# Decoder layer with a 32-expert MoE: biases kept resident and picked by a one-hot product, expert weights read in pairs of 4 MB

## What is computed

```python
logits = h.astype(jnp.float32) @ lw['w_router'].astype(jnp.float32) + lw['b_router'].astype(jnp.float32)
top_v, top_e = lax.top_k(logits, TOP_K)
gate = jax.nn.softmax(top_v, axis=-1).astype(h.dtype)
...
def run_block(args):
    xb, e = args
    gu = xb @ lw['w_gu'][e] + lw['b_gu'][e]
    gt = jnp.minimum(gu[:, :D_EXPERT], SWIGLU_LIMIT)
    up = jnp.clip(gu[:, D_EXPERT:], -SWIGLU_LIMIT, SWIGLU_LIMIT)
    act = (up + 1.0) * gt * jax.nn.sigmoid(SWIGLU_ALPHA * gt)
    return act @ lw['w_dn'][e] + lw['b_dn'][e]
```

## Time and profile before

| | us |
|---|---|
| median of 3 executions | 1600.88 (1596.57 to 1605.15) |
| the profiled execution, its own time | 1600.38 |
| its span in the trace | 1598.6 |
| TensorE busy in it | 1516.3 |
| VectorE, ScalarE busy | 482.5, 333.9 |
| items of the mixture of experts | from 640 to 1581 |

### The profile page before, as it was taken

The page is one execution under the profiler, slowest core; times in us unless marked ns, Lnnn a source line. Parts: engine busy times, 40 slices in busy tenths (PEclk is TensorE's granted clock), DMA queues, the critical chain, the costliest instruction groups (busy, mean ns, idle before and its releaser), DMA issues.

```text
span 1598.6 us, 24684 instructions
## 1 busy us (share of the span) xinstructions
PE 1516.3 (95%) x9777; PEld 797.6 (50%) x9777; DVE 482.5 (30%) x1079; ACT 333.9 (21%) x795; POOL 6.8 (0%) x13
## 2 busy tenths in 40 slices
PE   6999889999999999999999999999999999999996
PEld 4888885776677687333333333333333333333332
DVE  1566556323301024321222222222212212212224
ACT  2333551223311102111111111121111111111113
POOL 0000000000000000000000000000000000000000
PEclk8999999999999998999999999999999999999999
DMA  9748443534589964799999999999999999999991
GB/s 396 327 158 333 208 160 123 232 129 124 178 315 375 355 257 156 289 396 428 428 428 429 428 428 429 428 428 429 428 429 427 429 428 427 427 420 425 428 417 66
DMA packets 60258, 541.31 MB, mean 339 GB/s; under 512 B 7298, under 2 KB 11906, under 8 KB 29346
## 3 DMA queue, kind: packets, MB, share of 16 engines
q1 hardware_dynamic: 59474, 534.65, 81.3%
q0 software_dynamic: 720, 5.76, 0.9%
HBM read 533.54 MB, written 6.84 MB: 338 GB/s over the span
## 4 chain that ended last, share of the span: by engine, by line
PE 67%; DMA 21%; DVE 6%; issue 3%; SPq 2%; ACT 1%; ACTq 0%; DVEq 0%
DMA regC<-biases 20%; PE banks L605 14%; PE banks L558 10%; PE banks L1321 9%; PE banks L872 5%; PE banks L576 2%; PE banks L1154 2%; PE banks L508 2%; PE banks L1086 2%; PE banks L970 2%; DVE regA L693 2%; PE banks L533 2%; DMA ring<-wpre 1%; PE banks L805 1%; PE banks L1179 1%
## 5 line engine op out<-in xcount | busy, mean ns | idle before, releaser
L558 PE MATMUL banks<-ring,regA 128*64 128x512 f32 x2024 | 446.9, 594 | 0.7 <-ACT regA L630 0.7
L558 PEld LDWEIGHTS banks<-ring,regA 128*64 128x64 f32 x2024 | 142.5, 137 | 281.7 <-issue 280.7
L605 PE MATMUL banks<-ring,regC 128*64 128x512 f32 x1024 | 226.8, 595 | 1.4
L667 DVE TENSOR_TENSOR regB<-regB,banks 128x528 f32<-128x528 f32 x128 | 81.5, 699 | 334.1 <-PE banks L533 334.1
L605 PEld LDWEIGHTS banks<-ring,regC 128*64 128x64 f32 x1024 | 71.6, 137 | 136.0 <-issue 127.7
L633 ACT ACTIVATE regA<-regA 128x512 f32<-128x512 f32 x32 | 20.2, 631 | 538.0 <-DVE regA L688 538.0
L688 DVE TENSOR_SCALAR regA<-banks 128x512 f32<-128x512 f32 x32 | 22.1, 692 | 357.4 <-PE banks L576 357.4
L508 PE MATMUL banks<-regC,regA 128*64 128x512 f32 (+1 forms) x396 | 109.9, 677 | 0.0
L872 PE MATMUL banks<-hT,ring 128*128 128x264 f32 x384 | 86.5, 387 | 0.0
L872 PEld LDWEIGHTS banks<-hT,ring 128*128 128x128 f32 x384 | 72.6, 190 | 12.8 <-issue 0.4
L533 PE MATMUL banks<-regA,regC 64*128 64x264 f32 x512 | 71.6, 409 | 0.0
(11 more groups left out here) (476 smaller groups left out, 1538.0 us busy)
## 6 DMA issues: line engine op xcount, KB each, us to landing
ring<-w_gu SPq DMA_DIRECT2D x126, 2048.0 KB, 17.7
ring<-w_dn SPq DMA_DIRECT2D x64, 2048.0 KB, 15.0
ring<-wpre SPq DMA_DIRECT2D x41, 2048.0 KB, 13.3
ring<-kvT SPq DMA_DIRECT2D x64, 256.0 KB, 4.8
ring<-kv SPq DMA_DIRECT2D x64, 256.0 KB, 6.0
ring<-ssm SPq DMA_DIRECT2D x2, 2048.0 KB, 15.2
o_ssms<-ring POOLq DMA_DIRECT2D x2, 2048.0 KB, 8.2
regC<-w_gu SPq DMA_DIRECT2D x1, 2048.0 KB, 10.8
```

The lines of the kernel that those rows point to most:

```text
L558: mm = pe_mm(bank[x // 2][SLOT * (x % 2):SLOT * (x % 2 + 1), :], lhsT=hg[:, k % 4, SLOT * (k // 4):SLOT * (k // 4 + 1)], rhs=weights_k[:, ...
L605: mm = pe_mm(bank[5][SLOT * y:SLOT * (y + 1), :], lhsT=actT[:, m % 4, SLOT * (m // 4):SLOT * (m // 4 + 1)], rhs=ring[c][:, D * (m % 4) + H ...
L667: V.tensor_tensor(pair, pair, banks[:, b:b + 2, 0:T], ALU.add).then_inc(acc_added, 1)
```

## The change

- The six buffers become one tensor `ring_all`, so that two neighbours can be written as one pair of 4 MB: `pair[0]` is c0 and c1, `pair[1]` c2 and c3, `pair[2]` c4 and c5. From item 3 on, and for c2 to c5 of item 2, one DMA fills a pair, with rows of 32 KB. A pair is refilled when TensorE has read both its halves. Item 2 is written out too, so the loops of SP and TensorE start at 3.
- `w_dn` is read as rows 8p to 8p+7 in partition p, 32 KB in one piece. The intermediate columns follow: half y is now columns 8n + 4y + q, so the moving operand of the gate and up products (`own_columns`) takes 4 numbers, skips 4, takes 4.
- `brow` holds the gate and up biases of all 32 experts (two DMAs at the start, 2 x 128 KB); `load_bias` is gone. A stationary operand `pick` (64 partitions x 64), ones in expert e's row of each half, is made by one VectorE instruction an item, and the bias product is `pick` times `brow` over 32 partitions instead of one.
- `owner` says which expert an item has: two small copies of the identity at the start, one more copy and one small product for further items.

```diff
-        ring = [sb(f"ring{i}", [P, CH]) for i in range(RING)]
+        ring_all = sb("ring_all", [P, RING * CH])
+        ring = [ring_all[:, CH * i:CH * (i + 1)] for i in range(RING)]
+        pair = [ring_all[:, 2 * CH * i:2 * CH * (i + 1)] for i in range(RING // 2)]
...
-        wdn = t["w_dn"].rearrange("e (c p r) n -> e c p (r n)", c=2, p=P)
+        wdn = t["w_dn"].rearrange("e (p r) n -> e p (r n)", p=P)
+        def own_columns(v, y):
+
+            return v.rearrange("p (n y q) -> p n y q", y=2, q=4)[:, :, y, :]
+
...
-            def load_bias(e):
-                for u in range(2):
-                    sp.dma_start(brow[32 * u:32 * u + 1, :].rearrange("a (h n) -> a h n", h=2),
-                                 t["biases"][bass.ds(e, 1), :, HALF * u:HALF * (u + 1)]).then_inc(brow_in, 16)
+            def load_pair(i, e):
+                src = wgu[bass.ds(e, 1), :, 2 * CH * i:2 * CH * (i + 1)] if i < 2 else wdn[bass.ds(e, 1), :, :]
+                sp.dma_start(pair[i], src.rearrange("a p n -> p (a n)")).then_inc(slot_in[2 * i], 16)
...
-            load_bias(0)
-            def later_chunks(j, e):
-                for c in range(1, RING):
-                    sp.wait_ge(moe_read, j * 6 + (c - 5))
-                    load(c, e)
-                load_bias(e)
-
-            def first_chunk(j, e):
-                sp.wait_ge(moe_read, j * 6 - 5)
-                load(0, e)
+            for u in range(2):
+                sp.dma_start(brow[NE * u:NE * (u + 1), :].rearrange("e (h n) -> e h n", h=2),
+                             t["biases"][:, :, HALF * u:HALF * (u + 1)]).then_inc(stage("rest_in"), 16)
+
+            def later_pairs(j, e):
+                for i in range(1, 3):
+                    sp.wait_ge(moe_read, j * 6 + (2 * i - 4))
+                    load_pair(i, e)
+
+            def first_pair(j, e):
+                sp.wait_ge(moe_read, j * 6 - 4)
+                load_pair(0, e)
...
-            load_bias(1)
-
-            with sp.Fori(2, NE - 1) as j:
-                later_chunks(j, j)
-                first_chunk(j + 1, j + 1)
-            later_chunks(NE - 1, NE - 1)
+
+            sp.wait_ge(moe_read, 8)
+            load(1, 2)
+            later_pairs(2, 2)
+            first_pair(3, 3)
+            with sp.Fori(3, NE - 1) as j:
+                later_pairs(j, j)
+                first_pair(j + 1, j + 1)
+            later_pairs(NE - 1, NE - 1)
...
-                                       rhs=weights_k[:, HALF * x:HALF * (x + 1)],
+                                       rhs=own_columns(weights_k[:, D * (x // 2):D * (x // 2 + 1)], x % 2),
...
-                pe.wait_ge(brow_in, j * 32 + 32)
                 pe.wait_ge(acc_added, j * 4 + 5)
                 pe.wait_ge(sel_new, j + 2)
                 for x in range(4):
                     u, y = x // 2, x % 2
-                    mm = pe_mm(bank[u][SLOT * y:SLOT * (y + 1), :], lhsT=ones[32 * u:32 * u + 1, 0:SLOT],
-                               rhs=brow[32 * u:32 * u + 1, HALF * y:HALF * (y + 1)], start=False, stop=True, skip_group_check=True)
+                    mm = pe_mm(bank[u][SLOT * y:SLOT * (y + 1), :], lhsT=pick[NE * u:NE * (u + 1), :],
+                               rhs=own_columns(brow[NE * u:NE * (u + 1), :], y), start=False, stop=True, skip_group_check=True)
...
                 dve.wait_ge(gathered, j + 1)
+                V.tensor_scalar(pick[0:2 * NE, :], ones[0:2 * NE, 0:SLOT], owner[0:2 * NE, bass.ds(j, 1)], None, ALU.mult)
```

More of the change, by code:

```diff
@@ L254, in build_program @@
         cntc = cut(regA, 1600, 8)
-        e1h = cut(regA, 1608, NJ1)
         ge1 = cut(regA, 1657, NJ1)
@@ L267, in build_program @@
         act_ = cut(regA, 5400, 512)
+        pick = cut(regA, 5912, SLOT)
+        owner = cut(regA, 5976, NJ1)
+        e1h = owner[:, NE:NJ1]
         actT = cut(regC, 9700, 4, P)
@@ L501, in moe_loads @@
                         e = sp.value_load(items[0:1, bass.ds(j + 1, 1)], min_val=0, max_val=NE - 1)
-                        first_chunk(j, e)
-                        later_chunks(j, e)
+                        first_pair(j, e)
+                        later_pairs(j, e)
         def moe_tensor(pe, more_selections, more_products):
@@ L546, in item @@
                         pe.wait_ge(inputs_in, 96)
-                    elif isinstance(j, int) or c > 0:
-                        pe.wait_ge(slot_in[c], j * 16 + (moe_base[c] + 16))
-                    else:
-                        pe.wait_ge(slot_in[c], j * 16 + moe_base[c])
+                    elif isinstance(j, int) and (j < 2 or c < 2):
+                        pe.wait_ge(slot_in[c], 16 * min(j + 1, 2 if c == 0 else 3) + moe_base[c])
+                    elif c == 0:
+                        pe.wait_ge(slot_in[0], j * 16 + moe_base[0])
+                    elif c == 2:
+                        pe.wait_ge(slot_in[2], j * 16 + (moe_base[2] + 16))
                     for kk in range(2):
@@ L566, in item @@
                         if isinstance(j, int) and j == 0:
-                            pe.wait_ge(stage("rest_in"), 80)
+                            pe.wait_ge(stage("rest_in"), 112)
                             pe.wait_ge(stage("rg_copied"), 1)
                         scatter(j)
-                pe.wait_ge(brow_in, j * 32 + 32)
                 pe.wait_ge(acc_added, j * 4 + 5)
@@ L597, in item @@
                     c = 4 + m // 4
-                    if m % 4 == 0:
+                    if m % 4 == 0 and isinstance(j, int) and j < 2:
                         pe.wait_ge(slot_in[c], j * 16 + (moe_base[c] + 16))
+                    elif m == 0:
+                        pe.wait_ge(slot_in[4], j * 16 + (moe_base[4] + 16))
                     if m == 0:
@@ L612, in moe_tensor @@
             item(1)
-            K = for_items(pe, 2, item)
+            item(2)
+            K = for_items(pe, 3, item)
             pe.wait_ge(ytok_copied, K + 1)
@@ L1465, in more_products @@
                 pe.wait_ge(*once("e1h_ready"))
+                pe_mm(bank[7][NE:2 * NE, 32:32 + NX], lhsT=ident[0:NE, 0:NE], rhs=e1h[0:NE, 0:NX], start=True, stop=True)
                 pe_mm(bank[7][0:1, 8:8 + NX], lhsT=con[0:NE, C_E:C_E + 1], rhs=e1h[0:NE, 0:NX], start=True, stop=True).then_inc(stage("route"), 1)
@@ L2221, in _ @@
             link(V.tensor_scalar(slots, slots, -FAR, None, ALU.add))
+            for u in range(2):
+                link(V.tensor_copy(owner[NE * u:NE * (u + 1), 0:NE], ident[NE * u:NE * (u + 1), NE * u:NE * (u + 1)]))
             link(V.memset(selT[:, :], 0.0))
@@ L2283, in further_blocks @@
                 link(V.tensor_copy(items[0:1, 1 + NE:1 + NJ1], bank[7][0:1, 8:8 + NX]))
+                link(V.tensor_copy(owner[NE:2 * NE, NE:NJ1], bank[7][NE:2 * NE, 32:32 + NX]))
                 V.tensor_scalar(items[0:1, 0:1], bank[7][0:1, 2:3], float(NE), None, ALU.add).then_inc(once("items_ready")[0], 1)
```

3 lines of the change are left out of this document (1 added, 2 removed).

## The result

| | us |
|---|---|
| kernel before, median of 7 | 1600.88 (1596.38 to 1605.15) |
| changed kernel, median of 7 | 1585.72 (1584.2 to 1593.57) |
| ratio | 0.9924, 95% interval 0.9908 to 0.994 |
| profiled execution of the changed kernel, its own time | 1584.27 |
| its span | 1582.5 |

A forecast was written before the change was run, and what follows sets the result against it. The prediction took the weight transfers to set the pace at 29.70 us an item, TensorE 1.44 us behind. Terms -6.4 - 4.9 + 3.4 - 2.8 = -10.7 us from 1600.38 gave 1589.7, or 1590 as a median; range 1585 to 1595.

The forecast's parts named there:

- larger rows: Weight transfers, items 3 to 31: pairs save 24 packets an item and engine at 9.1 ns, 0.22 us; -6.4 us.
- bias transfers: Per-item bias reads dropped: two engines each lose two 2 KB packets, 0.17 us an item; -4.9 us.
- start: Item 2's weights, read as pairs, go out together and finish later in the queue: +3.4 us, ends 0 and 5.
- end: Last down products begin 2.6 us after the last landing instead of 5.4: -2.8 us, gained once.
- strided operand: Gate, up and bias products reading four columns, skipping four: no cost taken; upper bound 1.52 times.
- the ceiling of 434: Rival: packet cost goes entirely, transfers run at 434 GB/s, 28.96 us an item, 1580 us; chance 0.08.
- all 0.30 us: Upper end of the bias term: the whole missing 0.30 us an item goes, 8.7 us in sum.
- rival by which the engine is late anyway: Late engine not due to biases, or no 9.1 ns for long rows: 1595.1 without the bias term; joint chance 0.28.
- the sign that was set for the step: The bias step is wrong if one engine still lags by microseconds at the end.
- The two waits: TensorE's spare 1.05 us an item becomes waits of about 0.5 us at c0 and c2, replacing one of 1.4.
- rival of the clock: Waits in two places cost TensorE's clock, 1607 at one drop an item, or the queue runs dry, 1600; chance 0.07.
- that of the strided operand: Rival: TensorE reads strided weights more slowly and becomes the bound, 1604 at 10%, 1805 at 1.52 times; chance 0.07.

The follow-up runs named there:

- the pairs alone: Changed kernel with biases again read per item by two DMAs, waited for, and the one-partition bias product; pairs kept: 1596.83 us, ratio 0.9983.
- two transfers: Changed kernel plus two unused 4 KB bias reads an item behind `pair[2]`, which TensorE does not wait for: 1595.65 us, ratio 0.9981.
- its own run: Changed kernel with gate, up and bias products reading 512 neighbouring columns instead of four of every eight; output differs: 1583.0 us, ratio 0.99.
- the run with rows of 16 KB: Changed kernel with each pair filled by two 2 MB DMAs of 16 KB rows, still handed over as a pair: 1592.2 us, ratio 0.9951.
- the resident biases alone: Changed kernel with every item read in single 2 MB chunks of 16 KB rows as before, biases kept resident: 1583.35 us, ratio 0.9912.
- one extra transfer: Changed kernel plus one unused 4 KB bias read an item behind `pair[2]`, which TensorE does not wait for: 1588.58 us, ratio 0.9924.

## Why the prediction was right, and which terms were off

The time, 1585.72, lies 4.3 us under the forecast of 1590 and in its own range of 1585 to 1595; by the ratio it would be 1588.7. The mechanism is the one that was forecast: the queue sets the pace, a loaded engine lags in it, and both gains come as a shorter item. Of the terms, by their own steps:

| term | predicted | measured |
|---|---|---|
| larger rows, per item | 0.22 | 0.22 |
| larger rows, in sum | -6.4 | -5.5 |
| bias transfers, per item | 0.17 | 0.33 |
| bias transfers, in sum | -4.9 | -7.0 |
| start | +3.4 | +3.3 |
| end | -2.8 | -2.8 |
| strided operand | 0 | 0 |
| sum | -10.7 | -12.0 |

The measured sum stands against 12.8 in the loop and 12.2 by the ratio. It closes on the parts too: rows and start, 5.5 - 3.3 = 2.2, are the 2.3 us of the pairs alone.

**The rows.** The line through a 2 KB packet and a 16 KB packet gave 9.1 ns for each packet, and it holds for 32 KB: 0.224 us an item for 24, at most 0.03 of it for the three transfers less. Only the steady windows moved (428 to 432), and the ceiling of 434 was not reached.

**The bias transfers** are the mis-sized term. The step that failed is the packets' own time: "each of these carries two packets more: 2 x 84.5 ns = 0.17 us". Measured are 0.33. The packets do take 84.3 ns, and the two engines do carry two each, but each loses about twice that. The forecast's own upper bound was right within its rounding: "all 0.30 us" came from 12.58 MB at 428 GB/s, 29.40 us, and without bias transfers the item is 29.36. So the whole gap between the queue's rate and the item was the lagging engine, and "0.13 of the 0.30 us stays unexplained" was a real cost of the same transfers. Taking "the packets' own time, as it is worked out and the rest is not" was the mistake: the gap was measured, and only its cause was partly open. The rival by which the engine is late anyway is refuted, since its lag comes and goes with the rows on two engines. A spread of 2.9 us between first and last engine is left in the changed kernel, but it does not grow, and the last is 1.2 us behind the next, where it was 3.6 behind it at the end before; the sign that was set for the step, an engine that "still lags by microseconds at the end", did not allow for a lag that costs nothing an item.

One reading of the prediction holds only where it was used: that "a bias that has landed means that all of the item's weights have". In the earlier trace rows c5's last increment is 0.4 us ahead of the bias each time, but in items 2 to 5 the biases landed first, in item 2 at 708.00 for 708.38. The order of issue doesn't assure the order of landing.

**The count.** "Items 3 to 31 are 29", and both terms were multiplied by that. But the first items run at TensorE's 28.26 us, and a cost of the queue shows only later: the loop shows about 24 steady items' worth for the rows (5.45 / 0.224) and 21 for two transfers (7.0 / 0.33). The overcount hid half of the underestimate of the biases; it is in part luck that the sum came so near.

**The start** came as worked out, 3.3 us for 3.4. **The end** did too: the last increment for the last `pair[2]` stands at 1555.66, and the down products begin 2.6 us later, as forecast.

**The two waits** were put at about 0.5 us each. TensorE's timeline of the changed kernel:

```profile
1004.52 7.09 PE L619 MATMUL banks<-ring_all,regC 128*64 128x512 f32 x32
1011.73 3.65 PE L571 MATMUL banks<-ring_all,regA 128*64 128x512 f32 x16
...
1017.48 3.65 PE L571 MATMUL banks<-ring_all,regA 128*64 128x512 f32 x16
1021.45 7.09 PE L571 MATMUL banks<-ring_all,regA 128*64 128x512 f32 x32 [0.31 <-DMA ring_all<-w_gu]
1028.47 0.66 PE L588 MATMUL banks<-regC,regA 32*64 32x512 f32 x4
```

From the start of the down products to c0 are 7.21 us, where it was 6.91 without a wait: 0.3 at c0. From c1 to the bias product are 10.99, where it was 10.45: 0.5 at c2. The two are nearly the 0.88 us by which the item exceeds 28.26.

From 900 to 1200 the clock is at 1.00 in all kernels with these short waits, and at 0.98 in the two that wait for biases. The rival of the clock is refuted, and so is that of the strided operand, by its own run; the queue ran dry only at the start.

**What the sum did not say**, though its terms contained it: that the pairs bring nothing. Their 5.5 us of rows are lost again to the hand-over, 6.7 us in the loop by the run with rows of 16 KB. Of these 3.3 are the start; the end is 3.5, for with chunks the last down products begin 0.9 us ahead of the last landing (1556.38 and 1557.32) and with pairs 2.6 behind it. So the resident biases alone are as fast, 0.9912 against 0.9924. The end was counted as one gain of 2.8 us for the whole change; a tail with single chunks was not costed beside it, though the same rows would have allowed it.

## What to carry to other kernels

When a queue sets the pace, count the small transfers in it first, and ask on how many engines they run: two 4 KB reads an item cost more than halving the number of large packets returned, and they cost even if nobody waits for them. If the item takes longer than its bytes at the queue's own rate, compare how far the first and the last engine are apart early and late. Larger transfers buy a little rate and pay for it wherever the queue is short or the last piece is waited for, so put them only where the queue stays full. And a cost per item should be multiplied by the items in which the resource is the bound, which the intervals of one repeated issue show at a glance.

## What the runs showed of the hardware that was not expected

- One 4 KB transfer of two 2 KB rows on two engines costs the full queue 0.16 us an item where a row's own packet takes 84.3 ns, two cost 0.33, and the third and fourth 0.10 each. The same bytes over all 16 engines cost 0.13 us instead of 0.33.
- The loaded engines fall behind the others by what the rows cost, 0.32 us an item with two transfers, until the first and the last engine are about 7.6 us apart; up to then the queue's rate (431 GB/s) hides it, and afterwards it falls towards the pace (429 between 1200 and 1500, 427 being the pace).
- The delay of a loaded engine need not show for many items: with one extra transfer it took ten, six of them at TensorE's own pace.
- The price of a packet is the same from 2 KB to 32 KB rows: 9.1 ns by the line through the two shorter ones, 0.224 us / 24 = 9.3 ns between the two longer ones, with at most 1.1 ns of it for the fewer transfers.
- TensorE reads float32 columns in groups of four with gaps of four as fast as in one piece: 596 ns for both. The Trainium skill (SBUF — State Buffer, the note on cachelines) has lines of 16 bytes and full bandwidth for consecutive accesses to one line; four float32 fill such a line, and this run agrees.
